# A decoder layer with product-key experts: its row stream moved three steps ahead, and its last two half-steps and final sum taken apart

## The reference, cut to what matters

```python
def one_block(args):                        # h: 1024 tokens x 1024, 128*128 experts
    h_blk, idx_blk, g_blk = args            # 8 heads x 16 experts picked for each token
    u = jnp.take(expert_u, idx_blk, axis=0)
    act = jax.nn.gelu(jnp.einsum('thkd,td->thk', u, h_blk))
    vv = jnp.take(expert_v, idx_blk, axis=0)
    return jnp.einsum('thk,thkd->td', g_blk * act, vv)
...
x = x + g2[:, None, :] * peer(h2, ...)
return rmsnorm(x, final_g)                  # y = x * rsqrt(mean(x*x) + EPS) * g
```

## Time and profile before

| | |
|---|---|
| median of 3 runs | 3058.6 us |
| profiled execution | 3057.23 us, of which the trace spans 3055.5 us |
| mean granted TensorE clock | 0.983 |
| PE busy over the span | 2914.4 us (95%) |
| DVE busy | 2430.1 us (80%) |
| ACT busy | 1077.2 us (35%) |
| POOL busy | 1261.8 us (41%) |
| moved by DMA | 764.41 MB, mean 250 GB/s |

### The profile page before, as it was taken

The page is one execution under the profiler, slowest core; times in us unless marked ns, Lnnn a source line. Parts: engine busy times, 40 slices in busy tenths (PEclk is TensorE's granted clock), DMA queues, the critical chain, the costliest instruction groups (busy, mean ns, idle before and its releaser), DMA issues.

```text
span 3055.5 us, 50297 instructions
## 1 busy us (share of the span) xinstructions
PE 2914.4 (95%) x17341; PEld 2603.0 (85%) x17341; DVE 2430.1 (80%) x4849; ACT 1077.2 (35%) x1910; POOL 1261.8 (41%) x975
## 2 busy tenths in 40 slices
PE   6999999989999979988999999999999999999995
PEld 4998888878978878987898899999999998888884
DVE  5455333356469998978999999999999999999997
ACT  4221666621446655543222222222222222222222
POOL 0001000001049940014666666566656656665661
PEclk9999999999999989999999999999999999999997
DMA  6436333224221017898999999999999999999995
GB/s 240 153 111 196 105 111 109 82 103 173 97 70 58 28 46 215 248 295 313 360 354 366 354 355 344 352 349 349 335 346 353 346 345 357 364 349 354 357 345 219
DMA packets 348044, 764.41 MB, mean 250 GB/s; under 512 B 21020, under 2 KB 178808, under 8 KB 342400
## 3 DMA queue, kind: packets, MB, share of 16 engines
q0 software_dynamic: 115712, 419.48, 36.4%
q1 hardware_dynamic: 222928, 334.74, 32.6%
q10 hardware_dynamic: 9264, 8.39, 0.8%
HBM read 688.49 MB, written 74.03 MB: 250 GB/s over the span
## 4 chain that ended last, share of the span: by engine, by line
PE 26%; DVE 14%; issue 5%; DVEq 5%; PEld 5%; DMA 5%; POOL 1%; ACT 1%; PEldq 0%; POOLq 0%; ACTq 0%; SPq 0%
PE psum L2187 14%; PE psum L2180 12%; DVE ex_u_row L2409 4%; DVE acc L2422 4%; DVEq L2419 3%; DMA ex_v_row<-in_expert_v,ex_row 3%; PEld psum L1380 3%; PEld psum L1890 2%; DVE h_lo L2400 1%; DVE ex_c_lo L2429 1%; DVEq L2469 1%; DVE ex_g L2442 1%; DVE acc L2460 1%; DMA w_dram<-sc_w 1%; DVEq L2412 1%
## 5 line engine op out<-in xcount | busy, mean ns | idle before, releaser
L2140 POOL DMA_INDIRECT ex_u_row<-in_expert_u,ex_row x384 | 463.4, 1207 | 739.4 <-DVE ex_dot L2409 447.4
L2140 POOL DMA_INDIRECT ex_v_row<-in_expert_v,ex_row x384 | 537.2, 1399 | 123.7 <-issue 115.5
L2422 DVE SCALAR_TENSOR_TENSOR acc<-ex_v_row,ex_coef,acc 128x1024 f32<-128x1024 f32 x384 | 492.9, 1284 | 37.5 <-DMA ex_v_row<-in_expert_v,ex_row 11.5
L2409 DVE CUSTOM_DVE_ANT_0 ex_u_row<-ex_u_row,h_rows 128x1024 f32<-128x1024 f32 x384 | 467.9, 1219 | 5.0 <-DMA ex_u_row<-in_expert_u,ex_row 4.4
L2187 PE MATMUL psum<-ex_v_hi,ex_c_lo 128*128 128x512 f32 x1260 | 341.6, 393 | 19.0 <-DVE ex_v_lo L2404 19.0
L2187 PE MATMUL psum<-ex_v_lo,ex_c_hi 128*128 128x512 f32 x1260 | 338.0, 390 | 0.0
L2187 PE MATMUL psum<-ex_v_hi,ex_c_hi 128*128 128x512 f32 x1260 | 337.7, 390 | 0.0
L2180 PE MATMUL psum<-h_hi,h_lo 128*128 128x320 f32 x1712 | 288.7, 311 | 27.0 <-DVE h_lo L2400 13.1
L2180 PEld LDWEIGHTS psum<-h_hi,h_lo 128*128 128x128 f32 x1712 | 262.5, 188 | 35.5 <-issue 14.6
L2187 PEld LDWEIGHTS psum<-ex_v_hi,ex_c_lo 128*128 128x128 f32 x1260 | 234.7, 189 | 67.9 <-issue 21.7
L2180 PE MATMUL psum<-h_lo,h_hi 128*128 128x320 f32 x1712 | 289.9, 312 | 0.0
...
## 6 DMA issues: line engine op xcount, KB each, us to landing
ex_vn<-in_expert_v SPq DMA_DIRECT2D x64, 1024.0 KB, 7.9
ex_un<-in_expert_u_t SPq DMA_DIRECT2D x43, 1024.0 KB, 7.8
...
gm_wm<-in_w_mod SPq DMA_DIRECT2D x16, 1024.0 KB, 5.1
pj_raw<-in_w_in SPq DMA_DIRECT2D x11, 1024.0 KB, 8.7
ex_un<-in_expert_u_t SPq DMA_DIRECT2D x21, 512.0 KB, 7.6
...
```

Of the source, the lines that this page charges most:

```text
L2140: nc.gpsimd.indirect_dma_start(to[:], None, all_rows, bass.IndirectOffsetOnAxis(row[s][:, col:col + 1], 0)).then_inc(done, 16)
L2409: nc.vector.tensor_tensor_reduce(out=u_row[k % 3][:], in0=u_row[k % 3][:], in1=h_rows[:, k % 3, :], scale=1.0, scalar=0.0, op0=ALU.mult, o ...
L2422: nc.vector.scalar_tensor_tensor(out=to, in0=v_row[k % 3][:], scalar=coef[:, k:k + 1], in1=to, op0=ALU.mult, op1=ALU.add).then_inc(row_use ...
```

## The change

1. The row stream leads by three (`LEAD`): dense step c runs beside row step c+3. It catches up by one single pair more in every even step from 0 to 28 (15 pairs), in place of three halves (9 pairs) in steps 2, 6 and 10. Eight periods instead of three are written out (`PEELED`).
2. No rows are left for step 61; in step 60 the three dots of a 65th row step are left out.
3. Coefficients of step 63's second pair of tiles go to `last_c_hi`, `last_c_lo` (parts of `h`), and both V halves of steps 62 and 63 to `h`. So neither waits for shares of the step before.
4. `Finish`: totals of the row tiles 5, 6, 7 stand between the share adds of step 61; the kept tiles come in places 4 and 6 of `ORDER`; root and scaling follow at once; x is loaded in eight transfers, at four places of SP's queue; kept tiles have a result buffer and a semaphore of their own.

```diff
-    FIRST_PARTS = ((1, 2), (3, 4), (5, 6, 7), (8, 9), (10, 11), (12, 13), (14, 15, 16), (17, 18), (19, 20), (21, 22), (23, 24, 25), (26, 27))
-    PEELED = len(FIRST_PARTS) // PERIOD
+    LEAD, FIRST_PAIRS = 3, 3
+    PEELED = 8
+    def pairs_in(c):
+        q = FIRST_PAIRS + ROWS * c + min((c + 1) // 2, ROWS * LEAD - FIRST_PAIRS)
+        return range(q, q + (ROWS + 1 if c % 2 == 0 and c // 2 < ROWS * LEAD - FIRST_PAIRS else ROWS))
...
+    last_c_hi, last_c_lo = ([hh[:, 4 + e, 0:DENSE] for e in range(2)] for hh in (h.hi, h.lo))
+    def last_v(hh, j):
+        k = 2 * (PERIOD - 1 - j)
+        return hh[:, k:k + 2, :]
...
             load_v(sp, NI, 2)
+            sp.wait_ge(u_lo, blocks_before(NI, 3, blocks(3) + PRIME))
+            end.load(sp, 0, 2)
             load_v(sp, NI, 3)
             sp.wait_ge(hidden, ALL_HIDDEN)
-            end.sync(sp)
+            end.load_rows(sp)
+            sp.wait_ge(weighed, NSTEP * 4 + PRIME)
+            end.load(sp, 2, 4)
+            sp.wait_ge(summed, (NSTEP - 2) * NU + PRIME)
+            end.load(sp, 4, TT)
+            end.store(sp)
...
+            def split_last_v(j):
+                act.wait_ge(vn_in, (NI * PERIOD + j + 1) * 16)
                 act.wait_ge(hidden, ALL_HIDDEN)
-                nc.scalar.activation(h.hi[:, 0:2, :], v_flat(vn), ACT.Copy).then_inc(v_hi, 1)
+                nc.scalar.activation(last_v(h.hi, j), v_flat(vn), ACT.Copy).then_inc(v_hi, 1)
...
+                for n in range(NU):
+                    if n < blocks(j + 3):
+                        split_u(i, j + 3, n)
+                    rows(n)
+                    add(i, j, n, share_banks(j, units(j + 2)))
+                dve.drain()
...
+                for n in range(4):
+                    weigh(i, j + 3, n)
+                    if n < 3:
+                        rows(3 + n)
+                    if j % 2:
+                        lower(i, j + 3, n)
+                if pairs is not None:
+                    rows(6)
...
+            step(NI, 0, last=True)
             for n in range(4):
-                lower(NI, 3, n)
...
+                last_lower(n)
+            split_last_v(2)
+            end.vector(dve, add_last, lambda: split_last_v(3))
...
-    ORDER = (5, 6, 7, 2, 3, 4, 0, 1)
-    LOADS = (0, 2, 3, 5, 6, 8)
-    ADDS = {2: (0,), 3: (1,), 4: (2,)}
+    ORDER = (5, 6, 7, 2, 0, 3, 1, 4)
+    ADDS = {3: 0, 5: 1, 7: 2}
...
         dve.wait_ge(self.g_in[0], 16)
-        for k in range(TT + 3):
-            if k < TT:
-                total(k)
-            if 2 <= k < TT + 2:
-                average(k - 2)
-            if k >= 3:
-                norm(k - 3)
+        add_last(1, 0)
+        total(0)
+        add_last(1, 1)
+        total(1)
+        split_last()
+        add_last(1, 2)
+        average(0)
+        norm(0)
+        total(2)
+        average(1)
+        norm(1)
+        average(2)
+        norm(2)
+        for n in range(3):
+            add_last(2, n)
+        total(3)
+        for k in range(4, TT):
+            total(k)
+            average(k - 1)
+            norm(k - 1)
+        average(TT - 1)
+        norm(TT - 1)
```

More of the change, by code:

```diff
@@ L2189, in share @@
                     last.then_inc(summed, 1)
+                return last
             def u_split(i, j, e):
@@ L2227, in step @@
                     if kind == "share":
-                        share(s, KEPT + n, take(banks[n], ("share", j, n)), False, v)
+                        share(cs, KEPT + n, take(banks[n], ("share", j, n)), False, v)
                     else:
-                        share(s, n, core.bank[4 + 2 * n + dh], True, v)
+                        last = share(cs, n, core.bank[4 + 2 * n + dh], True, v)
+                        if not hiding and dh:
+                            last.then_inc(end.kept_done, 1)
             def among(g):
@@ L2256, in _ @@
             for j in range(PERIOD):
[L2257 removed]
+                step(NI, j, held, j < PERIOD - 2)
         @block.scalar
@@ L2342, in step @@
                 split_v(c + 1)
-                prepare_rows(*parts[1])
-                if hides:
-                    gelu(i, j + 3, hides)
-                for part in parts[2:]:
-                    prepare_rows(*part)
+                if pairs is None:
+                    prepare_rows(c + LEAD, 1, (j + LEAD + 1) % 2, last)
+                else:
+                    prepare_for(pairs, (3,))
+                for n in range(4):
+                    gelu(i, j + 3, n, hide_banks(j + 1))
+                    if pairs is not None and n:
+                        prepare_for(pairs, (n + 3,))
             def among(g):
@@ L2443, in weigh, with pair, add @@
                                         ALU.mult).then_inc(weighed, 1)
[L2445 removed]
+            def pair(c, k, last=False):
                 if k < 3:
                     row_dot(c, 3 + k)
[L2449 removed]
+                elif not last:
                     row_dot(c + 1, k - 3)
                 row_add(c, k)
[L2453 to L2478 removed]
+            def add(i, j, n, banks):
+                to = acc[:, KEPT + n, j % 2 * HALF:(j % 2 + 1) * HALF]
+                dve.wait_ge(summed, i * (PERIOD * NU) + (j * NU + n + 1 + PRIME))
+                nc.vector.tensor_tensor(to, core.bank[banks[n]], to, ALU.add).then_inc(added, 1)
             def among(g):
@@ L2510, in _, with step, rows @@
                 lower(0, 2, n)
-            def step(i, j, parts=None):
+            def step(i, j, pairs=None, last=False):
                 c = i * PERIOD + j
-                parts = parts or [(c + 2, 0), (c + 2, 3)]
-                shares(i, j, share_banks(j, units(j + 2)), blocks(j + 3), parts[0])
+                def rows(slot):
+                    if pairs is None:
+                        pair(c + LEAD, slot, last)
+                    elif slot < len(pairs):
+                        pair(*divmod(pairs[slot], ROWS))
+                for n in range(NU):
[4 more added lines that the diff above has]
+                dve.drain()
                 if j % 2:
@@ L2519, in step @@
                 split_v(c + 1)
-                hides(i, j, parts[1])
-                for r, k in parts[2:]:
-                    for n in range(3):
-                        pair(r, k + n)
+                for n in range(4):
+                    weigh(i, j + 3, n)
[3 more added lines that the diff above has]
+                        lower(i, j + 3, n)
+                if pairs is not None:
+                    rows(6)
             for c in range(PEELED * PERIOD):
-                j = c % PERIOD
-                step(c // PERIOD, j, [(p // 2, 3 * (p % 2)) for p in FIRST_PARTS[c]])
+                step(c // PERIOD, c % PERIOD, pairs_in(c))
             for i in periods(dve, PEELED, NI):
@@ L2566, in __init__, with load @@
             core.sem(f"fi_{n}") for n in ("summed", "squared", "averaged", "rooted", "normed", "stored"))
-    def x(self, k, n=1):
-        tiles, k = (self.xs[0], k) if k < 6 else (self.xs[1], k - 6)
-        return tiles[:, k, :] if n == 1 else tiles[:, k:k + n, :]
-    def sync(self, sp):
+    def load(self, sp, first, end):
+        for k in range(first, end):
+            c = self.ORDER[k]
+            sp.dma_start(self.xs[k][:], self.t.x2_dram[c * P:(c + 1) * P, :]).then_inc(self.x_in[k], 16)
```

183 lines of the change are left out of this document (86 added, 97 removed).

## The result

The changed kernel took 3065.4 us (median of 17 runs, 3061.3 to 3073.6), the kernel before 3059.2 us (17 runs, 3053.7 to 3061.8). The ratio is 1.0022, with a 95% interval of 1.0015 to 1.0028: slower by 6 to 7 us. The forecast was 3043 us, and its range ended at 3053. The profiled execution of the changed kernel, 3073.55 us with a span of 3071.6, was the longest of its 17, 8 us over their median; that of before stood within 2 us of its own.

What follows compares the result with a forecast made beforehand. PE was taken to bound most periods at 103.9 us, DVE the catch-up, late periods and end. From 3057.2 us, minus 1.3 (catch-up) and 14.2 (end), gave 3041.7; plus 1.4 to the median, 3043 us, range 3034 to 3053.

Steps and rivals of the forecast that it cites:

- The end: From step 61 to the last store: PE's long wait goes and DVE's line starts earlier, 14.2 us gained.
- the path to step 62's V on DVE: After step 61's V split at 2976.8: load, ACT and DVE split finish step 62's V at about 2988.
- The line of DVE's work behind `g2`: After the gate row lands at 2995: share adds, totals, scalings, V split, roots and drains in one line, 42.8 us.
- The roots: In the end's eight totals: each root, now waited for on the spot, exposes some 0.35 us, 2.8 us together.
- The catch-up: First 7.5 periods: 15 single extra pairs lose 14.3 us where nine lost 15.6, so 1.3 us gained.
- an extra pair costs 2.8 us, against a slack of 3.7 us a period: Catch-up periods of 26 pairs: DVE needs 105.8 us, 1.9 us over PE's 103.9.
- before's nine extra pairs, no longer paid: First three periods of the kernel before: the removed nine pairs had cost 15.6 us.
- the prediction's slower rival: Catch-up: extra pairs find no free row buffer and take 5.8 us each; 3087 us, chance 0.05.
- where DVE is the pace: Last period of the earlier trace: 99.0 us, plus 1.2 for a U split, gives an early period's 100.2.
- the rate of the transfers hardly moves: Catch-up: 26 pairs in 105.8 us need some 363 GB/s, where 362 were reached.
- one rival: Catch-up: POOL's gathers set the pace at 3.2 us a pair; 3049 us, chance 0.13.
- the wait of 10.55 us gone: Sign for the end: PE no longer waits 10.55 us for the lower part of step 62's V.

Runs made afterwards that it cites:

- e3: The changed kernel without its last three row steps, so with no extra pairs but the new end; 3032.0 us, 0.9906 of the kernel before.
- e8: The changed kernel run once more, unaltered, for a second profile; 3067.2 us, 1.0032 of the kernel before.
- e6: The changed kernel with each V load after the first bringing half its block; 3051.1 us, 0.9974 of the kernel before.
- the odd kernel: The changed kernel with its 15 single extra pairs at the end of odd steps 1 to 29 instead of even ones; 3052.3 us, 0.9979 of the kernel before.
- e11: The changed kernel with extra pairs in odd steps and V loads after the first halved; 3048.8 us, 0.9964 of the kernel before.

## Why the prediction was wrong, step by step

**The end was right, and 2.4 us too large.** 14.2 us were forecast and 11.8 came, the same in every kernel with that end and whole loads of V (69.1 or 69.2 us). The term that was off is the path to step 62's V on DVE. The prediction had DVE "free for it"; it wasn't: the last V row of step 60 arrived 3.37 us after DVE wanted it. ACT, in its fixed order, makes V's upper part behind the upper coefficients, which wait for DVE's weigh behind that row (4.59 us in the lines above), so the split began 13.5 us after step 60's V split, not 11.2, and V of step 63 and `g2`, which SP sends behind it, came 2.3 us later each. The line of DVE's work behind `g2` (42.8 forecast, 43.5 measured) and its parts held, and so did the statement that PE is not in it. The roots cost 0.27 us each, 0.35 forecast.

**The catch-up failed: its step "an extra pair costs 2.8 us, against a slack of 3.7 us a period".** Both numbers were off, each to the bad side. The profiles of e3 and of the changed kernel (with e8, the second one) settle it as a sum over the eight periods:

| | forecast | measured | e8 |
|---|---|---|---|
| DVE's extra busy time, 15 pairs | 36 (15 x 2.4) | 35.3 (805.95 - 770.68) | 35.2 |
| more waits for rows | 6 (the rest of 15 x 2.8) | 19.4 (26.9 - 7.5) | 14.2 |
| in small gaps (what the sum leaves) | 0 | 1.7 | 1.1 |
| slack that hides it | -27.8 (7.5 x 3.7) | -18.2 (20.5, less 2.3 still left) | -18.0 |
| cost | 14.3 | 38.2 | 32.5 |
| before's nine extra pairs, no longer paid | -15.6 | -13.8 | -13.8 |
| together | -1.3 | +24.4 | +18.7 |

Extra busy time was sized well. The *price of the waits for rows* was two to three times too small: 0.9 to 1.3 us a pair, not 0.4, so that a pair costs 3.4 to 3.8 us (50.5/15 and 56.4/15), up to where the prediction's slower rival began to decide (3.8 us; the size it gave, 5.8, was too much). And the *slack* was a third too large. It came from the last window of the earlier trace rows, "where DVE is the pace"; but that window is one of the shorter late periods, and the 1.2 us added for its missing U split is not all that an early one has more: e3 gives 831.3 - 20.5 = 810.8 us for eight, 101.4 us each, not 100.2. The 9.6 us between 27.8 and 18.2 would alone have put the sum at 3053 us, near no change.

Why were the waits mis-sized? The price was read off three pairs in a row, which had waited once for 0.69 us, and was carried over to fifteen pairs that each stand alone. Every step that runs one pair more pulls on three buffers whose turnaround (8.7 us in the timeline above) was already just within DVE's pace: e3 has 7.5 us of such waits with no extra pair at all. The prediction had said that "the rate of the transfers hardly moves" and so had counted nothing for it; the rate did not move (350 GB/s against 346 in e3 and 353 before), and the landing time hardly did: in e8 rows land in 6.7 and 7.2 us (U, V), in e3 in 6.6 and 7.2, and yet e8 waits 14 us more. So it is the more frequent use of the ring that runs into the turnaround; a shorter landing (e6) takes most of these waits away again. How a fourth row buffer would do was not tried.

**What holds a gather up.** The prediction has the means of a gather's issue on POOL in two stretches, 1.31 and 1.29 us; here too they are close, 498.36/384 = 1.30 us in e3 and 565.0/416 = 1.36 us in the changed kernel, with DVE 93% busy in both. Single gathers show what the means hide. In the changed kernel's eight periods all 28 gathers that were issued while DVE stood still took 0.93 or 0.94 us; of 367 whose issue began during a dot, a row add or a split of U or V, 366 ended 0.8 us after the end of that DVE instruction, and the 16 that began in a V split took 2.65 to 2.98 us. The Trainium skill (SBUF — State Buffer, "SBUF: two separate sides") says that a DVE instruction with two inputs in SBUF and a GpSimd instruction that reads SBUF shut each other out of a shared port for the whole instruction, whichever starts first. The trace agrees with it: these four read two or more tiles from SBUF, the gather reads its row numbers there (`ex_row`), and four gathers begun during a share add, with one input in psum, took 0.93 or 0.94 us.

The long issues stand where V rows come late. Taking the n-th V gather for the n-th row add, in e3 8 of 192 took 1.9 us or more, and 7 of these are all the V rows that DVE waited for (4.9 us). In the changed kernel such gathers have 9.3 of the 14.4 us of V waits, in the odd kernel 16.0 of 18.4 (30 gathers, 12 waited for), in e11 all 13.9. These are the odd kernel's longer waits, which the lighter load leaves. No run takes the hold away, so how much of each wait it makes is not shown; a hold of 1.0 us (1.97 less 0.94) can't be all of a wait of 2.9. The U rows' waits, 12.5 us in the changed kernel, are hardly marked so (1.7 us of them). Nor was POOL the pace of the catch-up, as one rival had it: it was busy for 565 of the 869 us.

**Of the signs** those for the end held (the wait of 10.55 us gone, DVE's unbroken run, `g2` 6.4 us behind its issue), but for PE's last matmul, which ended 50.7 us behind step 60's V split and not 40.5 to 49.5; those for the catch-up said that it was wrong: periods over 107 us, and PE waits over 2 us. The chances put 0.89 on faster; the case that came, slower by just over the 0.2% that can be told, had 0.05.
